# Dense expert activations kept on chip and gated in place, with the context's choices made first

## The reference, cut to what matters

```python
y, yc = even_mixer_2(hx, hc, ...)                 # ends in  concat(heads) @ w_out
x = x + g1 * y;  ctx = ctx + cg1 * yc
hx, hc = norm(x), norm(ctx)                       # with gain and shift of their own
q = (h @ w_q).reshape(T, 8, 2, 128)               # 8 heads, 2 sides
s = einsum('thpd,hpnd->thpn', q, sub_keys)        # 128 keys a side
sv, si = top_k(s, 16)                             # per token, head and side
cand = sv[:, :, 0, :, None] + sv[:, :, 1, None]   # 16 x 16 pairs
fv, fi = top_k(cand, 16)
idx = i1 * 128 + i2                               # 8 heads x 16 = 128 experts a token
g = softmax(fv)
act = gelu(einsum('td,ted->te', h, u[idx]))
f = einsum('te,ted->td', g * act, v[idx])
x = x + g2 * f[x's];  ctx = ctx + cg2 * f[ctx's]
```

## Time and profile before

| | us |
|---|---|
| three runs | 3846.37, 3844.53, 3841.45 |
| median | 3844.53 |
| profiled execution, its own time | 3843.3 |
| its span, first to last instruction | 3841.5 |
| PE busy in the span | 3526.2 (92%) |
| VectorE busy | 2646.4 (69%) |
| ScalarE busy | 1190.2 (31%) |
| GpSimd busy | 636.1 (17%) |
| moved by DMA | 882.90 MB, mean 230 GB/s |

### The profile page before, as it was taken

How to read it: one execution, slowest core, us unless ns; L and a number is a source line. 1 busy time by engine, 2 the same in 40 slices (tenths; PEclk the granted TensorE clock), 3 DMA queues, 4 the chain that set the end, 5 groups by cost and what they waited for, 6 DMA issues and landing times. The chain is left out here.

```text
span 3841.5 us, 61464 instructions
## 1 busy us (share of the span) xinstructions
PE 3526.2 (92%) x23498; PEld 3088.3 (80%) x23498; DVE 2646.4 (69%) x4823; ACT 1190.2 (31%) x1934; POOL 636.1 (17%) x564
## 2 busy tenths in 40 slices
PE   9998999989999879998499988788888999999999
PEld 9976999977988658886488766666676999998887
DVE  5665656646663464699888667677755698887887
ACT  4345334334442342110122100000035444543333
POOL 0000000001000010044555455555500000000000
PEclk9999999999999999999799999999999999999999
DMA  7652666634652113389899999999921576557776
GB/s 245 225 194 88 236 210 216 227 117 143 229 167 92 43 60 123 105 337 388 285 367 365 343 396 401 400 404 402 402 77 50 178 227 206 181 184 225 233 233 193
DMA packets 298398, 882.90 MB, mean 230 GB/s; under 512 B 32928, under 2 KB 99488, under 8 KB 297248
## 3 DMA queue, kind: packets, MB, share of 16 engines
q1 hardware_dynamic: 224416, 610.93, 47.0%
q0 software_dynamic: 73728, 268.47, 18.0%
HBM read 842.57 MB, written 36.70 MB: 229 GB/s over the span
## 5 line engine op out<-in xcount | busy, mean ns | idle before, releaser
L300 DVE TENSOR_TENSOR ring_lo<-ring,ring_hi 128x1024 fp32r<-128x1024 f32 x637 | 781.2, 1227 | 449.6 <-ACT ring_hi L294 429.7
L294 ACT ACTIVATE ring_hi<-ring 128x1024 fp32r<-128x1024 f32 x637 | 675.3, 1060 | 1032.4 <-PE banks L315 753.6
L325 PE MATMUL banks<-scratch,ring 128*128 128x256 f32 x2048 | 501.1, 403 | 118.7 <-DVE scratch L2766 118.5
L311 PE MATMUL banks<-h_parts,ring_hi 128*128 128x256 f32 x2312 | 575.9, 287 | 5.8 <-PEq L664 2.9
L325 PEld LDWEIGHTS banks<-scratch,ring 128*128 128x128 f32 x2048 | 403.7, 201 | 216.2 <-DVE scratch L2766 158.5
L312 PE MATMUL banks<-h_parts,ring_hi 128*128 128x256 f32 x2312 | 566.1, 283 | 0.0
L325 PE MATMUL banks<-h_whole,ring 128*128 128x256 f32 x2048 | 466.2, 385 | 60.9 <-ACT acts_out L2956 55.9
L325 PEld LDWEIGHTS banks<-h_whole,ring 128*128 128x128 f32 x2048 | 386.7, 192 | 117.5 <-ACT acts_out L2956 57.6
L311 PEld LDWEIGHTS banks<-h_parts,ring_hi 128*128 128x128 f32 x2312 | 442.0, 191 | 18.7 <-issue 17.8
L312 PEld LDWEIGHTS banks<-h_parts,ring_hi 128*128 128x128 f32 x2312 | 442.5, 191 | 0.3
L315 PE MATMUL banks<-h_parts,ring_lo 128*128 128x256 f32 x2312 | 325.2, 283 | 1.5 <-DVE ring_lo L300 1.4
(11 more groups left out here) (352 smaller groups left out, 6146.3 us busy)
## 6 DMA issues: line engine op xcount, KB each, us to landing
ring<-peer_u_dram SPq DMA_DIRECT2D x256, 512.0 KB
ring<-peer_v_dram SPq DMA_DIRECT2D x256, 512.0 KB
big<-mod_w_dram SPq DMA_DIRECT2D x96, 512.0 KB, 4.5
ring<-ffn_gate_dram SPq DMA_DIRECT2D x88, 512.0 KB
ring<-ffn_up_dram SPq DMA_DIRECT2D x88, 512.0 KB
ring<-ffn_down_dram SPq DMA_DIRECT2D x88, 512.0 KB
act_store<-acts_out SPq DMA_DIRECT2D x256, 128.0 KB
scratch<-act_store SPq DMA_DIRECT2D x256, 128.0 KB
```

The costliest lines, as they stand in the source:

```text
L294: self.nc.scalar.activation(self.hi[:, n % 2], self.ring[:, self.slot(j)], ACT.Copy).then_inc(self.count("tile_hi").sem, 1)
L300: self.nc.vector.tensor_tensor(self.lo[:, self.slot(j)], self.ring[:, self.slot(j)], self.hi[:, n % 2].bitcast(F32), ALU.subtract).then_in ...
L311: self.nc.tensor.matmul(out, w, b_hi, start=opens and m == 0, stop=False)
L325: ins = self.nc.tensor.matmul(out, self.ring[:, self.slot(j), c * P:(c + 1) * P], b, start=opens and m == 0, stop=opens and m == len(terms ...
```

## The change

Line numbers in this section are those of the changed kernel where they stand in rows of its order.

1. *Activations stay on chip.* `A` is a table of 128 x 128 x 256 values where G was; each gelu writes its tile there. `act_store`, its 128 stores and 128 loads are gone. A lies over the places of the queries, scores and choices, so ScalarE's gelus wait at tiles 40, 56, 72 and 80 until what lies there is done with.
2. *Gates in place, by halves.* There is no G and no copy by ScalarE. For each four tokens the gates are made for 64 of the first keys, then later for the other 64: 128 groups of 12 products of 128x64. VectorE multiplies A with them straight out of PSUM (`weigh`). The groups of the first half stand behind rises 86 to 127, those of the second behind falls 0 to 55; fall 64 waits for all of them. `fall` itself no longer waits for VectorE per tile.
3. *Context first.* Queries are made for the context with one load of the 16 tiles, and then for x with a second; its key scores, top sixteen and choices come before those of x. `spend` gives a step per 1450 columns (1150 before). Gathers of v begin with four steps of the first half of the tokens, then both halves alternate.
4. *Gather steps.* One or none (three in five) stands behind a group of the first half, one or two (each sixth) behind one of the second; all that are left stand together behind the last product with the gates.
5. *Output projection.* `out_by_stream` makes the context's sums first and norms it; the norm of x is then rounded into the former place of the other stream, and `both_experts` norms x itself.

```diff
-    parts, streams, sums, H = k.parts, (k.x, k.ctx), k.ps[:, 7, 0:T], KD // 2
...
+    parts, streams, sums, H = (k.parts[1], k.parts[0]), (k.ctx, k.x), k.ps[:, 7, 0:T], KD // 2
...
-    N, Q, NS, STEPS = NKEYS, 2 * HEADS, 58, T // 4
+    N, Q, STEPS, HALF = NKEYS, 2 * HEADS, T // 4, NKEYS // 2
+    U, V = 2 * Q, 2 * Q + NKEYS
...
-    G = k.region(0, NKEYS, T)
...
+    A = k.region(0, NKEYS, T)
...
+    AT_OWN_SCORES, AT_X_SCORES, AT_OWN_FOUND, AT_LEFT = 10240 // T, 14336 // T, 18432 // T, 20672 // T
...
+    order = [(0, t, p) for t in range(NT) for p in range(P)] + [(1, 0, p) for p in range(LEAD)]
+    order += [(1, t, p + LEAD * (1 - t)) for p in range(P - LEAD) for t in (1, 0)] + [(1, 1, p) for p in range(P - LEAD, P)]
...
+    EXP_OWN, SELECTED, FIRST_GATES = 30, 84, 86
+    gates_after = [[n for n in range(STEPS) if FIRST_GATES + n * (N - 1 - FIRST_GATES) // STEPS == e] for e in range(N)]
+    gates_under = [[n for n in range(STEPS, 2 * STEPS) if (n - STEPS) * (HALF - 8) // STEPS == r] for r in range(N)]
...
-            for j in range(R, Q + R):
-                k.fetch(sp, j, 0, wq[j] if j < Q else u[j - Q])
+            for m, stream in enumerate((k.x, k.ctx)):
+                sp.dma_start(k.kept_streams[m], stream[:]).then_inc(stored.sem, 16)
+            for j in range(R, U):
+                k.fetch(sp, j, 0, wq[j % Q])
             for e in range(N):
-                j = e + R
-                k.fetch(sp, Q + j, 0, u[j] if j < N else v[:, j - N])
-                sp.wait_ge(acted.sem, acted.after(e + 1))
-                sp.dma_start(k.act_store[e], k.acts[:, e % R]).then_inc(k.act_stored[e % R].sem, 16)
...
+                k.fetch(sp, U + e, 0, u[e])
+            for e in range(N):
+                k.fetch(sp, V + e, 0, v[:, e])
...
-                    if spent >= 1150:
-                        spent -= 1150
+                    if spent >= 1450:
+                        spent -= 1450
...
+                nc.vector.tensor_tensor(second[:, r], keys_in_twos.to_broadcast([P, 2, NKEYS, 2]),
+                                        of[:, 0].unsqueeze(2).to_broadcast([P, 2, NKEYS, 2]), ALU.is_equal).then_inc(marked.sem, 1)
+                nc.vector.tensor_tensor(in_half[:, r, 2], keys_in_twos[:, :, h * HALF:(h + 1) * HALF].to_broadcast([P, 2, HALF, 2]),
+                                        of[:, 1].unsqueeze(2).to_broadcast([P, 2, HALF, 2]), ALU.is_equal).then_inc(marked.sem, 1)
+                dve.wait_ge(marked.sem, marked.after(3 * n + 2))
+                nc.vector.tensor_tensor(in_half[:, r, 0:2], in_half[:, r, 2:3].to_broadcast([P, 2, 2, HALF, 2]),
+                                        of[:, 2:4].unsqueeze(3).to_broadcast([P, 2, 2, HALF, 2]), ALU.mult).then_inc(marked.sem, 1)
+                dve.wait_ge(marked.sem, marked.after(3 * n + 3))
+                nc.vector.tensor_tensor(in_half[:, r, 2], in_half[:, r, 2], of[:, 4].unsqueeze(2).to_broadcast([P, 2, HALF, 2]),
                                         ALU.mult).then_inc(marks_weighted.sem, 1)
+
+            def weigh(n):
+
+                h, n_of_half = n // STEPS, n % STEPS
+                acts = A[:, h * HALF:(h + 1) * HALF, n_of_half * B:(n_of_half + 1) * B]
+                dve.wait_ge(product.sem, product.after(n + 1))
+                nc.vector.tensor_tensor(acts, acts, k.ps[:, gate_bank(n), 0:B * HALF].rearrange("p (t n) -> p n t", t=B),
+                                        ALU.mult).then_inc(kept.sem, 1)
...
             for b in range(HEADS // 2):
-                for m in (1, 0):
-                    sixteen([t * HP + 4 * b + 2 * w + r for w in range(2) for t in range(NT) for r in range(2)], s[m], left, sv[m],
-                            si[m], lambda n, m=m: dve.wait_ge(moved.sem, moved.after(2 * (n % HP // 2) + 2 - m)))
+                level(1, 0, b)
+                if b < HEADS // 2 - 1:
+                    level(1, 1, b)
             dve.wait_ge(tokens_kept.sem, tokens_kept.after(2 * NT))
+            choices(1, 0)
+            level(1, 1, HEADS // 2 - 1)
+            LEVELS[1] = count
+            SETTLED[1] = choices(1, 1)
             for t in range(NT):
-                SETTLED[1] = choices(1, t)
+                for b in range(HEADS // 2):
+                    level(0, t, b)
+            LEVELS[0] = count
             for t in range(NT):
                 SETTLED[0] = choices(0, t)
             n = share(1)
-            for _ in range(4):
+            for _ in range(2):
                 token_step()
             dve.wait_ge(after.sem, after.after(n))
             FINAL = (SETTLED[0], SETTLED[0], share(0))
+            for _ in range(2):
+                token_step()
             part_weights()
-            for n in range(STEPS):
-                mark(n)
-                for _ in range(2 if n % 3 < 2 else 1):
+            for n in range(2 * STEPS + 1):
+                if n < 2 * STEPS:
+                    mark(n)
+                if n:
+                    weigh(n - 1)
+                for _ in range((n % 5 in (0, 2, 4)) if n < STEPS else 1 + (n % 6 == 0)):
                     token_step()
-            before = step
-            for e in range(N):
-                weigh(e)
-                while (step - before) * N < (e + 1) * (2 * TOKEN_STEPS - before):
-                    token_step()
+            while step < len(order):
+                token_step()
             dve.wait_ge(restored.sem, restored.after(32))
...
-                    for m in (0, 1, 3):
-                        last = nc.tensor.matmul(k.ps[:, n % R, t * P:(t + 1) * P], marks[:, n % 2, 2, t // 2, :, t % 2],
-                                                marks[:, n % 2, m, t // 2, :, t % 2], start=m == 0, stop=m == 3)
+                    for m in range(3):
+                        last = nc.tensor.matmul(k.ps[:, gate_bank(n), t * HALF:(t + 1) * HALF], second[:, n % 2, t // 2, :, t % 2],
+                                                in_half[:, n % 2, m, t // 2, :, t % 2], start=m == 0, stop=m == 2)
                 last.then_inc(product.sem, 1)
 
             def fall(r):
 
-                pe.wait_ge(weighted.sem, weighted.after(r + 1))
-                k.whole(pe, Q + N + r, [(sums[:, c], c, hidden[:, r % R]) for c in range(KD)], False).then_inc(done.sem, 1)
+                k.whole(pe, V + r, [(sums[:, c], c, A[:, r]) for c in range(KD)], False).then_inc(done.sem, 1)
...
+            for e in range(1, N):
                 rise(e)
...
-            for e in range(NS, N):
-                rise(e)
-                if 0 <= e - NS - GATES_LAG < STEPS:
-                    gates(e - NS - GATES_LAG)
+                if e == SELECTED:
+                    for w in range(3):
+                        pe.wait_ge(after.sem, after.after(FINAL[w]))
...
+                for n in gates_after[e]:
+                    gates(n)
             pe.wait_ge(kept.sem, kept.after(STEPS))
+            pe.wait_ge(acted.sem, acted.after(N))
             k.open_banks(range(4))
             for r in range(N - 1):
+                if r == HALF:
+                    pe.wait_ge(kept.sem, kept.after(2 * STEPS))
                 fall(r)
-            pe.wait_ge(weighted.sem, weighted.after(N))
+                for n in gates_under[r]:
+                    gates(n)
...
-                act.wait_ge(done.sem, done.after(Q + e + 1))
-                act.wait_ge(k.act_stored[e % R].sem, k.act_stored[e % R].after(16 * (e // R)))
-                nc.scalar.activation(k.acts[:, e % R], k.ps[:, 4 + e % 2, 0:T], ACT.Gelu).then_inc(acted.sem, 1)
+                if e == AT_OWN_SCORES:
+                    act.wait_ge(top.sem, top.after(LEVELS[1]))
+                if e == AT_X_SCORES:
+                    act.wait_ge(top.sem, top.after(LEVELS[0]))
+                if e == AT_OWN_FOUND:
+                    act.wait_ge(after.sem, after.after(SETTLED[1]))
+                if e == AT_LEFT:
+                    act.wait_ge(after.sem, after.after(SETTLED[0]))
+                    nc.scalar.activation(weights[0], weights[0], ACT.Exp).then_inc(exps.sem, 1)
+                act.wait_ge(done.sem, done.after(U + e + 1))
+                nc.scalar.activation(A[:, e], k.ps[:, 4 + e % 2, 0:T], ACT.Gelu).then_inc(acted.sem, 1)
...
-    out_by_stream(k, a.even_out, cat, [k.mods[:, 0, 2 * KD:3 * KD, m] for m in range(2)], norm_of(k, 0, 1, 0), first(a.peer_q[0]),
+    split_input(k, cat[:, :, T:2 * T], k.parts[1], first(a.even_out))
+    out_by_stream(k, a.even_out, cat, [k.mods[:, 0, 2 * KD:3 * KD, m] for m in (1, 0)], norm_of(k, 0, 1, 1), first(a.peer_q[0]),
...
-    both_experts(k, a, 0, norm_of(k, 0, 1, 1))
+    both_experts(k, a, 0, norm_of(k, 0, 1, 0))
```

More of the change, by code:

```diff
@@ L2595, in _ @@
             pool.wait_ge(stored.sem, stored.after(32))
-            for n in range(2 * TOKEN_STEPS):
-                t, p = divmod(n, P) if n < TOKEN_STEPS else (n % NT, (n - TOKEN_STEPS) // NT)
-                if n < TOKEN_STEPS and p == 0:
+            pool.wait_ge(scaled.sem, scaled.after(KD))
```

(55 more changed lines are left out.)

225 lines of the change are left out of this document (87 added, 138 removed).

## The result

| | us |
|---|---|
| changed kernel, median of four runs | 3869.51 (3867.29 to 3873.62) |
| kernel before, on the same chip | 3845.45 (3841.45 to 3848.26) |
| ratio | 1.0065, 95% interval 1.0047 to 1.0082 |
| profiled execution, changed | 3868.35, span 3866.6 |

A forecast was written before the change was run, and what follows sets the result against it. The prediction took DMA bandwidth, not VectorE or TensorE, to set the end in falling. Gather steps ending 34 us later plus 3 for a slow PE restart gave +37 on 3843.3: 3880 us, 8-in-10 range 3826 to 3920.

The forecast's parts named there:

- rival A: The forecast itself: gather steps left over run alone on five buffers at the end; 3880 us (3862 to 3905), chance 0.50.
- 53 steps behind: At 2334 us, VectorE's new order has 231 gather steps done where the kernel before had 284.
- the last product with the gates: End of all gate groups in both_experts, forecast at 2334 us; 281 of 512 gather steps follow it.
- the prediction's own signs of being wrong: Last gate group done before 2300, lone gathers keeping 1.31 us, or v starving with PE still falling at the end.
- gate group: PE's 12 gate products of 64 columns, assumed as dear as a group of 128 columns: 0.74 us.
- a gather beside them: Gathers while PE's 72 remaining falls load v: left 262 GB/s, 2.0 us each, 137 gathers.
- lone gathers: The last 139 gathers, after PE's last fall, at 1.55 us each: 215 us.
- Rival C: Narrow gate groups cost PE half, 47 us less before falling's later part: 3833 or 3799 us, chance 0.18.
- the tail: After 2334 us: 274 us of falls with gathers beside them, then 215 us of gathers alone; steps end at 2824.
- the loop: Five gather buffers cycling through VectorE's step, GpSimd's issue and the landing: a period of 1.48 to 1.68 us.
- By bandwidth alone the change is worth nothing: After 2334 us, 182.5 MB left at 400 GB/s takes 456 us, ending at 2790 as before the change.
- the prediction's c: Period of one gather running alone at the end, taken as 1.55 us; 1.4 to 1.7 gave 3862 to 3905.

The follow-up runs named there:

- gates twice: Changed kernel with each gate product issued a second time, same result: 3909.52 us, one run.
- quarter steps: Changed kernel with VectorE's v step working on 256 of the 1024 columns, the rest of the context's sums left out: 3814.63 us, one run.
- the last version: Changed kernel with six buffers, more gather steps under the gates, v paced to the gathers, and 15 more steps where VectorE waited before the gates: 3752.84 us, ratio 0.9764.

## Why the prediction was right, and where its terms were off

The side, the mechanism and the place of the loss were as forecast in rival A: 53 steps behind, a lone tail of gathers, PE idle beside it. The sum came out 11.9 us too high by span, and that it came so near is in part luck: the last product with the gates came 37 us before the forecast, the stretch from there to the last step took 26 us longer, and the stages behind took 2 less than allowed. One of the prediction's own signs of being wrong, a last gate group before 2300, was met. The terms:

| term | forecast | measured |
|---|---|---|
| x's choices ready; asked for | 1840; 1881 | 1850.9; 1877.5 (VectorE then waits from 1862.4 to 1879.3 for the exponential) |
| falls begin | 2092 | 2074.4 |
| gate group | 0.74 us | 0.36 |
| last product with the gates, over | 2334 | 2297.2 |
| 72 falls, one | 274 us, 3.8 | 253 us, 3.46, and one wait of 3.3 |
| a gather beside them | 2.0 us | 2.08 |
| lone gathers | 139 at 1.55 = 215 | 159 at 1.645 = 262 |
| stages behind (before: 1051.4) | +3 | 1052.7: +1.3 |

*The gate group* is the step that failed: "I take 0.74, nearest to that row". The fp32 product with 8 columns, 0.15 us, was no guide to the bf16 products of 64, 0.03 us each. The rule that I had set aside, of the Trainium skill, TensorE: Matmul & The Clock Gate, section Back-to-back issue gap, gave 0.3, and the trace, 0.36 / 12 = 30 ns a product, is near it. Rival C's condition was thus met, and its faster result did not come: of its price of 47 us 37 were won at 2297, and the tail took them back. With the price that I had assumed (gates twice) the kernel takes 3909.5 us, not 3880: the last product came at 2342, where I had 2334, and from there the steps took 517 us, as in the changed kernel, where I had 490. So where the assumed price holds, the forecast is 29 us too low by span.

*The tail* was mis-sized twice. The falls kept their unhindered beat, although the DMA engines were full: it was the gathers that gave way (2.08 us each), and they had 21 us less to run beside the falls, so 20 more of them were left to run alone (five of these the sum had left out as landed). And a lone gather took 1.645 us, near the upper end of 1.48 to 1.68 that the loop gave. The loop was a part of the cause: of 1.645 - 1.31 = 0.33 a sixth buffer took 0.2, quarter steps all. The rest is GpSimd's own pace, 1.12 us an issue and 0.32 between two with six buffers; its issues are longer than 0.94 us where they start inside a two-input step.

*"By bandwidth alone the change is worth nothing"* held as a sum of bytes, and missed what the change opens: from 1855 to 2297 the DMA engines move 252 to 308 GB/s while VectorE waits 60.3 us. Gather steps put there cost 31.4 / 51 = 0.62 us each, where they cost 1.645 at the end. That is a large part of the gain of the last version, and the handwritten order of the change left it unused. Steps moved into the selection do the same: a step per 1150 columns takes back the whole loss.

Worked out again, the prediction's c from 1.4 to 1.7 gives 3859 to 3901, not 3862 to 3905; the measured time lies in both.

The swapped output projection moved nothing ahead of the stage: the stage behind it begins at 1470.4, where it began at 1470.8.

## What to carry to other kernels

When a change takes a shared transfer away, look where the steps of the other user of bandwidth now stand in the order. Work that is left to run alone at the end goes at the pace of its own chain (buffers, issues, steps), not at bandwidth's. Estimate the period by that chain, here (step + 0.82 + landing) / (buffers - 1), and compare it with the issuing engine's own pace; the longer one counts. With five buffers the loop gave 1.48 to 1.68 and 1.645 was measured; with six it gives 1.19 to 1.34, and GpSimd's pace of 1.44 was measured. A price taken from a row of another type and width is a guess: keep both ends, and carry each end through to the last instruction, since what is won ahead may only lengthen the tail.

## What was unexpected of the hardware

- An indirect issue on GpSimd takes 0.94 us; one that starts within a VectorE step with two inputs of 1024 columns, 0.1 us or more behind its start, ends about 0.82 us after that step, up to 1.99 in all. One that started before the step or in its first 0.1 us is not slowed.
- Beside one-input steps of 0.75 us, issues that had begun before the step and were not over ended about 0.12 after it, up to 1.30 us in all.
- With the DMA engines full (400 GB/s), loads of v tiles kept the falls' pace of 3.46 us and the indirect gathers took what was left, 2.08 us each instead of 1.32. In the kernel before it was otherwise for u: 4.09 us a rise at 415 GB/s (1754 to 1775), where stores of activations ran too, and PE waited 2.0 us of the 21 for the tiles. What makes the difference was not tested.
